# Sample attention: the key bias spread over the heads by TensorE instead of by DMA replicas

## The reference, cut to what matters

```
I[t, s]  = sum over 8 index heads of w[t, h] * relu(q_idx[t, h] . k_idx[s])   (keys after t are -inf)
sel      = top 256 of I[t, :]                                  # one selection per token, for all 8 heads
score    = q . k * 64 ** -0.5 - slope_h * (pos_t - pos_s)      # only the selected keys take part
out      = softmax(score) @ v                                  # 8 heads share 2 key/value heads
```

## Time and profile before

| what | value |
|---|---|
| median of 3 runs | 2839.86 us |
| the profiled execution's own time | 2838.16 us |
| its span (first to last instruction) | 2836.4 us |
| TensorE busy | 2640.2 us, 93% |
| VectorE busy | 1928.7 us, 68% |
| ScalarE busy | 831.6 us, 29% |
| mean granted TensorE clock | 0.977 of full speed |

### The profile page before, as it was taken

The page is one execution under the profiler, slowest core; times in us unless marked ns, Lnnn a source line. Parts: engine busy times, 40 slices in busy tenths (PEclk is TensorE's granted clock), DMA queues, the critical chain, the costliest instruction groups (busy, mean ns, idle before and its releaser), DMA issues. The chain is left out here.

```text
span 2836.4 us, 31368 instructions
## 1 busy us (share of the span) xinstructions
PE 2640.2 (93%) x11706; PEld 1462.7 (52%) x11706; DVE 1928.7 (68%) x3926; ACT 831.6 (29%) x1363; POOL 48.4 (2%) x65
## 2 busy tenths in 40 slices
PE   7987999899999999999999998799999868999988
PEld 5743444454544545454545454554555546676653
DVE  4309899996797989897989998218995014454442
ACT  4222223322323233323333423412121433221210
POOL 0000000000000000000000000010000100000000
PEclk9998999999999999999999999899999989999999
DMA  7111111111111111110101011042324849453307
GB/s 212 35 37 34 45 42 39 35 44 38 41 42 31 41 35 36 31 44 29 44 26 44 23 40 34 5 164 83 105 98 126 228 185 306 157 183 104 130 30 31
DMA packets 212168, 215.33 MB, mean 76 GB/s; under 512 B 76208, under 2 KB 198704, under 8 KB 208368
## 3 DMA queue, kind: packets, MB, share of 16 engines
q1 hardware_dynamic: 203824, 153.13, 18.9%
q0 software_dynamic: 7072, 60.18, 6.8%
q10 hardware_dynamic: 1120, 0.00, 0.1%
HBM read 157.56 MB, written 55.72 MB: 75 GB/s over the span
## 5 line engine op out<-in xcount | busy, mean ns | idle before, releaser
L787 PE MATMUL attn_ps_r<-xnT,early 128*128 128x424 f32 (+2 forms) x2464 | 993.4, 543 | 30.5 <-ACT early L638 15.7
L115 DVE TENSOR_SCALAR_CACHE_REDUCE early<-early 128x384 uint8<-128x384 f32 (+13 forms) x462 | 681.8, 1476 | 11.5
L787 PEld LDWEIGHTS attn_ps_r<-xnT,early 128*128 128x128 f32 x2464 | 443.1, 191 | 441.9 <-issue 424.3
L1095 PE MATMUL samp_ps_r<-xnT,early 128*128 128x424 f32 (+1 forms) x800 | 286.8, 521 | 6.2 <-PEq L89 6.2
L657 ACT ACTIVATE attn_probT<-attn_ps_p 128x512 f32<-128x512 f32 (+1 forms) x288 | 151.8, 571 | 405.4 <-PE attn_ps_p L832 405.3
L1662 PE MATMUL merge_ps_y<-merge_w_out,merge_merged 128*128 128x512 f32 (+1 forms) x544 | 235.0, 592 | 1.2 <-DVE merge_merged L1791 1.2
L1095 PEld LDWEIGHTS samp_ps_r<-xnT,early 128*128 128x128 f32 x800 | 152.5, 191 | 138.2 <-issue 137.6
L715 DVE SCALAR_TENSOR_TENSOR early<-attn_relu,early 128x512 f32<-128x512 f32 (+3 forms) x266 | 182.1, 685 | 30.9 <-ACT attn_relu L674 3.4
L638 ACT ACTIVATE early<-attn_ps_r 128x424 f32<-128x424 f32 (+1 forms) x130 | 67.9, 523 | 427.2 <-PE attn_ps_r L787 425.9
L817 PE MATMUL attn_ps_s<-kT,qT 64*128 64x512 f32 (+3 forms) x640 | 162.9, 588 | 26.0 <-DVE early L744 19.0
L832 PE MATMUL attn_ps_p<-ident,prob 128*128 128x128 f32 x1088 | 155.7, 282 | 25.5 <-ACT prob L693 25.4
(11 more groups left out here) (236 smaller groups left out, 2309.7 us busy)
## 6 DMA issues: line engine op xcount, KB each, us to landing
rest_t<-early SPq DMA_DIRECT2D x144, 212.0 KB, 1.9
early<-in_w_in SPq DMA_DIRECT2D x104, 256.0 KB, 3.4
early<-in_x_prompt SPq DMA_DIRECT2D x16, 512.0 KB, 3.9
merge_x<-in_x_prompt SPq DMA_DIRECT2D x8, 1024.0 KB, 5.0
out_y_prompt<-merge_y POOLq DMA_DIRECT2D x16, 512.0 KB, 5.0
rest_t<-early SPq DMA_DIRECT2D x36, 208.0 KB, 2.1
merge_ga<-rest_t SPq DMA_DIRECT2D x7, 1024.0 KB, 10.8
merge_gc<-rest_t SPq DMA_DIRECT2D x7, 1024.0 KB, 9.5
```

The lines of the kernel that those rows point to most:

```text
L115: self.v.done(self.nc.vector.tensor_scalar(self.hits, self.x, limit, None, op, ALU.add, accum_out=self.count))
L787: ins = nc.tensor.matmul(ps_r[:, 0:width], w_rest[:, n % 2, k, :], c.xnT[:, k, t0:t0 + width], start=(k == 0), stop=(k == KC - 1))
L1095: ins = nc.tensor.matmul(ps_r[:, i % 2, 0:width], w_rest[:, (slot0 + j) % 2, k, :], c.xnT[:, k, t0:t0 + width], start=(k == 0), stop=(k == ...
```

## The change: what it does, and the diff

The DRAM scratch tensor, its store, the eight replica loads and their semaphores go. In their place a matrix of zeros and ones, `spread`, 64 x 64 for each sequence, is made once on VectorE at the start of the stage: row r (a token), column (head, t) is one where r is token t of that sequence. `replicate(p)` is now a function on TensorE: for each of the 9 chunks of a pair, two matmuls (one for each sequence) of `spread` with the bias tile `score` write the bias of 128 rows to PSUM, two chunks deep. `add(p)` on VectorE is now 9 instructions, each adding a chunk from PSUM to `prob` and carrying the maximum on.

```
             def _(tensor queue):
+                def replicate(p):
+                    for q in range(NC + 1):
+                        e = p * (NC + 1) + q
+                        if q == 0:
+                            pe.wait_ge(biased, 1)
+                        if p == 2 and q == 0:
+                            pe.wait_ge(rest_kept, len(steps))
+                        if e >= 2:
+                            pe.wait_ge(biased_one, e - 1)
+                        width = 512 if q < NC else ST
+                        for u in range(2):
+                            ins = nc.tensor.matmul(ps_bias[p][u * 64:u * 64 + 64, e % 2, 0:width],  spread[:, 2 * p + u, :],
+                                                   score[0:ST, q * 512:q * 512 + width], start=True, stop=True)
+                        ins.then_inc(replicated, 1)
...
                 score_pair(1)
-                project_rest(RESTS[2], RESTS[4])
+                project_rest(RESTS[2], RESTS[3])
+                replicate(0)
+                project_rest(RESTS[3], RESTS[3] + 2)
+                replicate(1)
+                project_rest(RESTS[3] + 2, RESTS[4])
                 weigh_pair(0)
                 score_pair(2)
+                replicate(2)
                 turn_att(0)
                 weigh_pair(1)
                 score_pair(3)
+                replicate(3)
                 turn_att(1)
...
             def _(pool queue):
-                def replicate(p):
-                    for u in range(2):
-                        src = a["bias_scratch"][2 * p + u].unsqueeze(0).to_broadcast([NH, DT, KEYS])
-                        pool.dma_start(replicas[p % 2][u * 64:u * 64 + 64, :], src).then_inc(replica_in[p % 2], 16)
...
-                pool.wait_ge(biased, 1)
-                pool.dma_start(a["bias_scratch"].rearrange("b t k -> (b t) k"), score[0:ST, :]).then_inc(bias_out, 16)
-                pool.wait_ge(bias_out, 16)
-                replicate(0)
-                replicate(1)
                 pool.wait_ge(rest_done, len(steps))
                 keys(2)
                 values(1)
-                pool.wait_ge(added, 1)
-                replicate(2)
-                pool.wait_ge(added, 2)
-                replicate(3)
                 pool.wait_ge(weighted, NC + 1)
                 keys(3)
...
             def _(vector queue), start of the stage:
+                v.done(nc.vector.tensor_scalar(ints[:, 2:3], ints[:, 0:1], 3, None, ALU.logical_shift_right))
+                v.done(nc.vector.tensor_copy(slope[:, 1:2], ints[:, 2:3]))
+                v.done(nc.vector.tensor_scalar(same_b[:], step8[0:ST, :], slope[0:ST, 1:2], None, ALU.is_equal))
+                for b in range(DB):
+                    v.done(nc.vector.tensor_scalar(spread[:, b, :].rearrange("r (h t) -> r h t", t=DT),
+                                                   same_t[0:ST, :].unsqueeze(1).to_broadcast([ST, NH, DT]),
+                                                   same_b[:, b:b + 1], None, ALU.mult))
...
                 def add(p):
                     dve.wait_ge(s_kept, (p + 1) * (NC + 1))
-                    dve.wait_ge(replica_in[p % 2], 32 * (p // 2 + 1))
-                    nc.vector.tensor_tensor_reduce(out=prob[:, p % 2, :], in0=prob[:, p % 2, :], in1=replicas[p % 2][:],
-                                                   scale=1.0, scalar=-3.0e38, op0=ALU.add, op1=ALU.max,
-                                                   accum_out=largest[:, p:p + 1]).then_inc(added, 1)
+                    for q in range(NC + 1):
+                        e, width = p * (NC + 1) + q, 512 if q < NC else ST
+                        dve.wait_ge(replicated, e + 1)
+                        if e:
+                            dve.wait_ge(biased_one, e)
+                        keys = prob[:, p % 2, q * 512:q * 512 + width]
+                        nc.vector.tensor_tensor_reduce(out=keys, in0=ps_bias[p][:, e % 2, 0:width], in1=keys, scale=1.0,
+                                                       scalar=chunk_max[:, q - 1:q] if q else -3.0e38, op0=ALU.add,
+                                                       op1=ALU.max, accum_out=chunk_max[:, q:q + 1]).then_inc(biased_one, 1)
```

More of the change, by code:

```diff
@@ L922, in stage_sample_attention @@
         relu = m.sb("relu", [P, 2, 512])
-        att = m.sb("att", [P, 2, HD])
+        att = [c.iksT, m.sb("att", [P, HD])]
         found = m.sb("found", [P, 3, PAIRS])
+        chunk_max = m.sb("chunk_max", [P, NC + 1])
+        same_b = m.sb("same_b", [ST, DB])
+        spread = m.sb("spread", [ST, DB, NH * DT])
         ps_t = m.psum("ps_t", [P, 2, 4, P])
@@ L941, in stage_sample_attention @@
         probT = relu[:].rearrange("p s (n r) -> p s n r", n=4)
-        largest, negmax, rowsum = found[:, 0], found[:, 1], found[:, 2]
+        negmax, rowsum = found[:, 1], found[:, 2]
         attT = c.qs[0:HD].rearrange("p a n t -> p (a n) t")
-        replicas = (bias, score)
+        ps_bias = (ps_i, ps_i, ps_r, ps_r)
         (tabled, iw_out, spread_in, ready, rowed, idx_in, masked, positioned) = [m.sem(n) for n in (
@@ L950, in stage_sample_attention @@
         (k_turned, k_kept, multiplied, s_kept) = [m.sem(n) for n in ("k_turned", "k_kept", "multiplied", "s_kept")]
-        (biased, bias_out, added, maxed, exped, p_turned, p_kept, weighted, normalised, att_turned, att_kept,
+        (biased, maxed, exped, p_turned, p_kept, weighted, normalised, att_turned, att_kept,
          att_out) = [m.sem(n) for n in (
-            "biased", "bias_out", "added", "maxed", "exped", "p_turned", "p_kept", "weighted", "normalised",
+            "biased", "maxed", "exped", "p_turned", "p_kept", "weighted", "normalised",
             "att_turned", "att_kept", "att_out")]
@@ L960, in stage_sample_attention @@
         v_in = [m.sem(f"v_in{p}") for p in range(PAIRS)]
-        replica_in = [m.sem(f"replica_in{s}") for s in range(2)]
+        replicated, biased_one = m.sem("replicated"), m.sem("biased_one")
         win = a["w_in"].rearrange("l (k p) n -> (l p) k n", p=P)
@@ L1077, in _ @@
                     pool.wait_ge(v_in[p], 32)
-                for n in range(2):
-                    pool.wait_ge(replica_in[n], 64)
                 pool.dma_reset()
@@ L1197, in weigh @@
                             pe.wait_ge(att_kept, p - 1)
+                        else:
+                            pe.wait_ge(biased_one, 2 * (NC + 1))
                     for n in range(4 if q < NC else 1):
@@ L1218, in turn_att @@
                     pe.wait_ge(normalised, p + 1)
-                    nc.tensor.transpose(ps_i[0:HD, p % 2, P:2 * P], att[:, p % 2, :], c.ident[:]).then_inc(att_turned, 1)
+                    nc.tensor.transpose(ps_i[0:HD, p % 2, P:2 * P], att[p % 2][:], c.ident[:]).then_inc(att_turned, 1)
                 project_rest(0, RESTS[0])
@@ L1438, in add @@
                     dve.wait_ge(s_kept, (p + 1) * (NC + 1))
-                    dve.wait_ge(replica_in[p % 2], 32 * (p // 2 + 1))
-                    nc.vector.tensor_tensor_reduce(out=prob[:, p % 2, :], in0=prob[:, p % 2, :], in1=replicas[p % 2][:],
-                                                   scale=1.0, scalar=-3.0e38, op0=ALU.add, op1=ALU.max,
-                                                   accum_out=largest[:, p:p + 1]).then_inc(added, 1)
-                    dve.wait_ge(added, p + 1)
-                    nc.vector.tensor_tensor(negmax[:, p:p + 1], largest[:, p:p + 1], slope[:, 1:2], ALU.mult
+                    for q in range(NC + 1):
[7 more added lines that the diff above has]
+                                                       op1=ALU.max, accum_out=chunk_max[:, q:q + 1]).then_inc(biased_one, 1)
+                    dve.wait_ge(biased_one, (p + 1) * (NC + 1))
+                    nc.vector.tensor_tensor(negmax[:, p:p + 1], chunk_max[:, NC:NC + 1], slope[:, 1:2], ALU.mult
                                             ).then_inc(maxed, 1)
@@ L1455, in normalise @@
                             r = slice(u * 64 + kv * 32, u * 64 + kv * 32 + 32)
-                            last = nc.vector.tensor_scalar(att[r, p % 2, :], ps_i[r, p % 2, kv * HD:(kv + 1) * HD],
+                            last = nc.vector.tensor_scalar(att[p % 2][r, :], ps_i[r, p % 2, kv * HD:(kv + 1) * HD],
                                                            rowsum[r, p:p + 1], None, ALU.mult)
```

3 lines of the change are left out of this document (1 added, 2 removed).

## The result

The changed kernel takes 2853.11 us, the median of five runs (2851.91 to 2855.36); five runs of the kernel before beside it gave 2839.0 (2837.76 to 2840.79). The ratio is 1.0052, 95% interval [1.0039, 1.0064]: slower by 14.1 us, where the forecast was 15.5. The profiled execution took 2852.96 us, 14.8 more than the one before.

The account below looks back on a forecast made before the run. TensorE, busy 93% of the span, was taken as the bound. The terms 32.8 - 19.4 - 1.4 + 2.2 + 1.3 = +15.5 us gave a forecast of 2855 us, range 2845 to 2865.

Parts of the forecast that it names:

- four blocks of bias products: On TensorE, two among rest steps, two behind score pairs: 8.2 us each, +32.8 us in all.
- K3's wait: TensorE before score_pair(3): the 19.39 us wait goes, as replicas 2 and 3 no longer precede K3 in POOL's queue.
- pair 3's scores at full clock: score_pair(3) on TensorE: without the slow start after the wait, 16.6 us instead of 18.0, 1.4 us less.
- exp(2) ahead of pair 3's copies: Start of score_pair(3): exp(2) delays ScalarE's copies of turned keys, so TensorE waits; +2.2 us.
- clock after that gap: After TensorE idles about 2.5 us for exp(2), a lowered clock adds 1.3 us, with 0 as the other end.
- K2's wait: TensorE before score_pair(2): the 6.28 us wait stays, since SP's loads still start with K2; 0 us change.
- The loop over two buffers: In each block, chunk e+2 waits for VectorE to have read chunk e: 1.98 us for two chunks.
- The lower bound: TensorE's own pace in the blocks: 0.89 us a chunk, 7.4 us a pair, 29.6 us in all.
- the serial rival: In the blocks, a chunk's two products run one after the other: 25 us more, 2880 us; chance 0.04.
- the 0.1 us that the prediction put on a change of tiling: By the skill's drain rule, about 0.1 us for each of 8 tiling changes would make the sum 1 us longer.
- The rival of a late K3: Before score_pair(3), slower gathers leave a K3 wait of 4 to 14 us: 2857 to 2867 us; chance 0.10.
- The rival that the relieved engines bring K2 in time: Start of score_pair(2): 6.28 us of wait goes and full clock comes, 8.3 us less, 2847 us; chance 0.10.

Follow-up runs that it names:

- the four-deep kernels: Changed kernel with four chunks in PSUM instead of two, the scores' banks added: 2857.6 us; with another order of banks 2849.6 us.
- The kernel with early replicas: Kernel before, with POOL issuing the replicas of pairs 2 and 3 ahead of its wait for the last rest step: 2821.9 us.
- the changed kernel with late merge loads: Changed kernel with SP's 3.1 MB of loads for the merge held back until pair 2's keys are turned: 2846.2 us.
- the three versions that keep replicas and have this gap: Kernel before, replicas early: 2821.9 us; that with merge loads late: 2815.6 us; changed kernel with pairs 0, 1 by DMA replicas: 2837.3 us.
- the changed kernel with exp(2) behind: Changed kernel with exp(2) placed behind the copies of pair 3 on ScalarE instead of ahead of them: 2850.2 us.
- the version with both moves and exp(2) behind: Kernel before with replicas early, merge loads held back until pair 2's keys are turned, and exp(2) behind pair 3's copies: 2818.4 us.

## Why the prediction was right

| term | forecast, us | measured, us |
|---|---|---|
| four blocks of bias products | +32.8 | +32.2 |
| K3's wait | -19.4 | -19.4 |
| pair 3's scores at full clock | -1.4 | -1.6 |
| exp(2) ahead of pair 3's copies | +2.2 | +2.3 |
| clock after that gap | +1.3 | 0 |
| K2's wait | 0 | +1.2 |
| stage begins later | 0 | +0.8 |
| the rest | 0 | -0.9 |
| sum | +15.5 | +14.6 |

The measured column is worked out on TensorE's timeline, from the rows above against the earlier trace rows. Pair 3's scores: 2287.95 to 2306.62 without the 2.27 is 16.4, against 18.0. The rest is weigh_pair(1) (13.73 against 14.38), pair 2's scores (18.29 against 18.59), weigh_pair(3) (14.72 against 14.92) and 0.3 among the rest steps. That the sum comes within 1 us is in part luck: 1.3 us too much for the clock, 0.6 for the blocks and 0.9 in the rest stand against 2.0 us for K2 and the start that were put at nothing.

- **The blocks.** The loop over two buffers was forecast at 1.98 us for two chunks and measured 1.94; the four-deep kernels showed that it is this loop. The lower bound, 0.89 us a chunk taken from the score products, was a little high: with four buffers two chunks take 1.72. "Only two chunks fit in PSUM" was the kernel's choice, not a limit: the four-deep kernels found two more places in the scores' banks. VectorE's pace by itself was put too low, at 0.80 us a chunk where four buffers show 0.90; with two the loop hides it. The products of a chunk do run beside each other, so the serial rival falls. The Trainium skill, "TensorEngine Tiling (Array Packing)", section "Key Properties", has the array drain when the tiling changes. Here, from a block's last chunk of 64 columns to the next product in another tiling are 0.21 us (2187.60 to 2187.81, 2267.46 to 2267.67), less than the 0.26 of the 64 keys in the scores, where the tiling stays: no drain is seen here either. No row of this case has the 0.1 us that the prediction put on a change of tiling.
- **K3.** The kernel with early replicas shows the cause. K3's two halves were issued at 2240.70 and 2241.94 and landed 31.8 and 36.3 us after that, the later one some 51 us after the last rest step (54 forecast), and TensorE came 61 us after that step, as forecast. The rival of a late K3 falls.
- **K2.** The prediction said that its wait stays, since SP's loads share the engines with it; holding these back took most of it away, 5.8 of 7.5 us. The rival that the relieved engines bring K2 in time falls: there was no relief at that moment, 280 GB/s against 303 before. By the Trainium skill, "DMA: Bandwidth & Descriptors", section "Queues, rings and completion order", an engine takes turns between the rows that have work. The runs agree in that SP's row takes a share from POOL's: 7.47 us of wait beside it, 1.64 without it. That it goes by turns, none of them shows. The 1.2 us more are no effect of the change that can be told: the changed kernel's other profile has 6.94, the other versions without late loads 6.59 to 8.15.
- **exp(2).** Place, cause and size came as worked out.
- **The clock after exp(2)'s gap** is the step that failed: 1.00 in the changed kernel, where 1.3 us had been added (with 0 as the other end). In the changed kernel with late merge loads (above), and in the three versions that keep replicas and have this gap, it did fall to 0.90 after the same 2.27 us. Which of the two comes is not explained.
- **The start.** The stage's first rest step starts at 1838.42 instead of 1837.64, ahead of anything the change touches. The eight matrices (2.42 us, not the 1.6 of the copies) are hidden: the wait for POOL behind them fell from 11.10 to 7.93 us. One thing there was not foreseen: in every kernel whose bias is spread on TensorE alone, the page table at the stage's start lands later (16.9 us after its issue instead of 8.1 here), and VectorE's start with it, by 9.6 us. TensorE runs rest steps for 59 us then and does not wait for it; why it lands later is not known.

## What to carry to other kernels

A transfer that costs time is first asked what stands behind it in its queue: here moving four replica loads ahead of a wait was worth 18 us, and replacing them by TensorE work, on the engine that is busy 93%, cost 32 to gain 19. Here work that was moved to the busiest engine was paid in full, among the rest steps as well as behind the scores; none of the kernels placed it in one of that engine's own gaps, so what it costs there is not shown. The loop of two engines over two buffers had to be priced by its round trip (1.94 us for two chunks), not by the slower of the two (1.80).

## What the runs showed of the hardware that was not expected

- Full DMA engines moved very different amounts, by what they moved: 208 GB/s with replicas among the gathers, 221 with replicas and the rest steps' stores alone (early replicas, 2181 to 2210, share 0.97), 280 with K2, V1 and SP's loads (share 0.90), 284 with V1, K3 and SP's loads, 400 to 405 with gathers once most of SP's loads were over. At this last rate, by an estimate from these rows, the replicas' bytes would have been priced at half their time.
- VectorE's instruction on a chunk lasts 0.75 us, but one starts every 0.90 even when TensorE is not waited for: a read of the maximum, 0.08 us, follows each, and the next waits for the one before it (`biased_one`), whose maximum it carries on. With TensorE at 0.86 a chunk, VectorE falls behind by 0.04 us a chunk, some 0.3 us over a block (an estimate from these two), which four buffers cover.
- After gaps of the same length at the same place (2.27 us for ScalarE) the granted clock of the next 15 to 17 us was 1.00 in some kernels and 0.90 in others, a difference of 1.5 us. After the gap of 2.81 us ahead of weigh_pair(3) it was 0.88 to 0.90 in most, 1.00 (13.7 us instead of 14.7) in the changed kernel with exp(2) behind, and 0.82 in the version with both moves and exp(2) behind.
